# A filter network's third weight stacked on 128 partitions, x loaded in pieces, and a chunk evicted earlier, in a two-block transformer kernel

## The reference

```
h = x * (1 + sc1) + sh1;   z = h @ w_in + b_in
u, v = gelu(z[:, 0:1024]), gelu(z[:, 1024:2048]);   v = layer_norm(v)
f = sin(freq * (feats @ w1 + b1))          # 256 x 33 @ 33 x 64
f = sin(freq * (f @ w2 + b2))              # 64 x 64
f = f @ w3                                 # 64 x 4096: direction, order, 1024 channels
filt = f.reshape(256, 2, 2, 1024) * window[:, None, None, :]
spectrum(order n) = rfft of filt[:, 0, n] forwards and filt[:, 1, n] backwards
```

## Time and profile before

| | |
|---|---|
| median of 3 runs | 2676.2 us (2675.57 to 2677.15) |
| the profiled execution | 2677.23 us |
| its span in the trace | 2675.9 us |
| PE busy | 2630.5 us (98%) |
| DVE busy | 1840.9 us (69%) |
| ACT busy | 1291.8 us (48%) |
| moved by DMA | 598.48 MB, mean 224 GB/s |

### The profile page before, as it was taken

How to read it: one execution, slowest core, us unless ns; L and a number is a source line. 1 busy time by engine, 2 the same in 40 slices (tenths; PEclk the granted TensorE clock), 3 DMA queues, 4 the chain that set the end, 5 groups by cost and what they waited for, 6 DMA issues and landing times.

```text
span 2675.9 us, 32016 instructions
## 1 busy us (share of the span) xinstructions
PE 2630.5 (98%) x12713; PEld 2194.3 (82%) x12713; DVE 1840.9 (69%) x1919; ACT 1291.8 (48%) x1566; POOL 37.5 (1%) x62
## 2 busy tenths in 40 slices
PE   6999999999999999999999999999999999999999
PEld 2679988888888888888888888888888888988887
DVE  6878879887886654577776867765554665566565
ACT  2345544444444444555555544444444565545463
POOL 0000000000000000000000000000000000000000
PEclk9999999999999999999999999999999999999999
DMA  9999778888878865565556555555565556634554
GB/s 296 343 327 336 266 253 305 287 302 314 313 248 276 278 204 188 182 215 191 199 188 195 192 184 192 185 189 189 190 212 189 189 187 164 187 115 153 199 183 142
DMA packets 295800, 598.48 MB, mean 224 GB/s; under 512 B 21716, under 2 KB 46943, under 8 KB 285551
## 3 DMA queue, kind: packets, MB, share of 16 engines
q1 hardware_dynamic: 285952, 561.56, 62.6%
q0 software_dynamic: 5552, 25.23, 2.8%
q10 hardware_dynamic: 4158, 9.79, 1.0%
HBM read 586.05 MB, written 10.49 MB: 223 GB/s over the span
## 4 chain that ended last, share of the span: by engine, by line
PE 95%; DVE 3%; ACT 1%; DMA 1%; issue 1%; SPq 0%; ACTq 0%; DVEq 0%
PE ps L893 27%; PE ps L895 26%; PE ps L894 26%; PE ps L1016 2%; PE ps L1000 2%; PE ps L1002 2%; PE ps L1003 2%; PE ps L1092 1%; DVE w_lo L2261 1%; DMA raw<-in_w_ada 1%; PE ps L1435 1%; PE ps L1437 1%; PE ps L1436 1%; DVE ada_acc L2289 1%; PE ps L1085 0%
## 5 line engine op out<-in xcount | busy, mean ns | idle before, releaser
L2261 DVE TENSOR_TENSOR w_lo<-raw,w_hi 128x1024 fp32r<-128x1024 f32 x870 | 1051.3, 1222 | 698.4 <-ACT w_hi L1581 696.4
L1581 ACT CAST w_hi<-raw 128x1024 fp32r<-128x1024 f32 x870 | 909.0, 1051 | 1070.0 <-PE ps L895 964.9
L893 PE MATMUL ps<-w_lo,x_hi 128*128 128x512 f32 x2592 | 1020.8, 394 | 7.1 <-DVE x_lo L2416 3.4
L895 PE MATMUL ps<-w_hi,x_lo 128*128 128x512 f32 x2592 | 1011.9, 390 | 0.0
L894 PE MATMUL ps<-w_hi,x_hi 128*128 128x512 f32 x2592 | 1011.4, 390 | 0.0
L893 PEld LDWEIGHTS ps<-w_lo,x_hi 128*128 128x128 f32 x2592 | 488.5, 188 | 112.5 <-DVE x_lo L2416 5.0
L895 PEld LDWEIGHTS ps<-w_hi,x_lo 128*128 128x128 f32 x2592 | 488.2, 188 | 102.6
L894 PEld LDWEIGHTS ps<-w_hi,x_hi 128*128 128x128 f32 x2592 | 488.5, 188 | 100.7 <-issue 1.4
L2289 DVE SCALAR_TENSOR_TENSOR ada_acc<-raw,cond,ada_acc 128x2048 f32<-128x2048 f32 x64 | 150.1, 2346 | 1.0 <-DVE ada_acc L2289 0.5
L893 PE MATMUL ps<-w_lo,pooled_hi 128*128 128x512 f32 x384 | 150.2, 391 | 0.0
L895 PE MATMUL ps<-w_hi,pooled_lo 128*128 128x512 f32 x384 | 149.5, 389 | 0.0
(11 more groups left out here) (408 smaller groups left out, 2223.7 us busy)
## 6 DMA issues: line engine op xcount, KB each, us to landing
raw<-in_w_m SPq DMA_DIRECT2D x128, 1024.0 KB, 5.1
raw<-in_w_in SPq DMA_DIRECT2D x72, 1024.0 KB, 6.4
raw<-in_w_ada SPq DMA_DIRECT2D x64, 1024.0 KB, 5.5
raw<-in_pool_w_in SPq DMA_DIRECT2D x64, 1024.0 KB, 5.2
raw<-in_w_ada SPq DMA_DIRECT2D x64, 512.0 KB, 5.7
raw<-in_pool_w_out SPq DMA_DIRECT2D x32, 1024.0 KB, 5.0
raw<-in_ple_w_gate SPq DMA_DIRECT2D x32, 1024.0 KB, 5.1
raw<-in_mla_w_in SPq DMA_DIRECT2D x24, 1024.0 KB, 5.1
```

The lines of the kernel that those rows point to most:

```text
L893: mm(bank, xh, wl, start=start, stop=False)
L895: ins = mm(bank, xl, wh, start=False, stop=stop)
L1581: nc.scalar.copy(by_ktile(st, w_hi[st.half_slot(j, half)][:, 0:n]), raw_half(st, j, half)).then_inc(hi_split, 1)
L2261: tt(by_ktile(st, w_lo[slot][:, 0:n]), raw_half(st, j, half), by_ktile(st, w_hi[slot][:, 0:n].bitcast(F32)), ALU.subtract).then_inc(lo_spl ...
```

## The change

- The third weight `w3` now has 128 partitions of 2048 columns: the forward half on partitions 0 to 63, the backward half on 64 to 127. The second weight `w2`, its bias and the frequencies are loaded twice side by side, so that the second layer comes out on 128 partitions, its lower and upper halves equal. ACT takes three sines: `hid_dif` (upper half negated, in two operations) and `hid_sum`. Each filter product is then one matmul per 128 tokens with 128 rows, for all four chunks. `filter_weights` and `w3_sum` go.
- ACT issues ten small loads and one of `w3`; POOL waits for the ten, then issues the other half of `w3`, `window` and `dft`. Each of the four loads of x waits for one more of DVE's adds (`ada_added` 2 to 5) in place of `w3`.
- DVE's order up to the end of group 0 changes.
- In `in_vu` DVE evicts chunk 2 ahead of the last three pieces of w_ada, `gelu(2)` and the rounding of the table go behind the fourth half piece of `in_h` on ACT, and the table's split goes into `in_h` on DVE. The order of the loads is as before.

```diff
-    ("in_vu", 1, [("w", "awaaa")]), ("in_h", 2, A2), ...
+    ("in_vu", 1, [("wa", "waaa")]), ("in_h", 2, A2), ...
...
-    w3 = at("w3", 148, [4 * W1])
-    w3_sum = at("w3_sum", 120, [2 * W1])
+    w3 = at("w3", 156, [2 * W1])
...
+        pool.wait_ge(hidden_in, 160)
+        pool.dma_start(w3[HID:P, :], a["hy_w3"][0][:, 2 * W1:4 * W1]).then_inc(w3_back_in, 16)
         for dst, src in matrices:
             pool.dma_start(dst, src).then_inc(matrices_in, 16)
-        pool.wait_ge(w3_in, 64)
...
         for c in range(4):
+            pool.wait_ge(ada_added, 2 + c)
             pool.dma_start(res[:, :, cols(c)], x_rows[:, :, cols(c)]).then_inc(x_loaded, 16)
...
-        pe.wait_ge(hidden_in, 96)
+        pe.wait_ge(hidden_in, 160)
...
-        mm(ps[0:HID, 0, 0:S], w2[0:HID, :], hid_arg[0:HID, :], start=True, stop=True).then_inc(hid_mm, 1)
+        mm(ps[:, 0, 0:S], w2[0:HID, :], hid_arg[0:HID, :], start=True, stop=True).then_inc(hid_mm, 1)
...
-                bwd = w3[0:HID, 2 * W1 + col:2 * W1 + col + CH]
-                if it == 0:
-                    mm(bank, hid_arg[0:HID, tokens], w3[0:HID, 0:CH], start=True, stop=False)
-                    ins = mm(bank, (hid_neg if d else hid_arg)[0:HID, tokens], bwd, start=False, stop=True)
-                else:
-                    part = bwd if d else w3_sum[0:HID, col:col + CH]
-                    ins = mm(bank, hid_arg[0:HID, tokens], part, start=True, stop=True)
+                ins = mm(bank, (hid_dif if d else hid_sum)[:, tokens], w3[:, col:col + CH], start=True, stop=True)
...
-        pe.wait_ge(w3_in, 64)
+        pe.wait_ge(w3_in, 16)
+        pe.wait_ge(w3_back_in, 16)
...
-        pe.wait_ge(w3_ready, 2)
...
-            (w2[0:HID, :], a["hy_w2"][0], hidden_in), (hid_rows[0:1, :], a["hy_b1"], hidden_in),
-            (hid_rows[1:2, :], a["hy_b2"], hidden_in), (hid_rows[2:3, :], a["hy_freq"], hidden_in),
-        ]
+        ] + [(dst[:, HID * n:HID * (n + 1)], src, hidden_in) for n in range(2) for dst, src in (
+            (w2[0:HID, :], a["hy_w2"][0]), (hid_rows[0:1, :], a["hy_b1"]), (hid_rows[1:2, :], a["hy_b2"]), (hid_rows[2:3, :], a["hy_freq"]))]
...
-        for part in range(4):
-            columns = slice(part * W1, (part + 1) * W1)
-            act.dma_start(w3[0:HID, columns], a["hy_w3"][0][:, columns]).then_inc(w3_in, 16)
+        act.dma_start(w3[0:HID, :], a["hy_w3"][0][:, 0:2 * W1]).then_inc(w3_in, 16)
...
-                nc.scalar.activation(hid_neg[0:HID, :], hid_arg[0:HID, :], ACT.Sin, scale=-1.0)
-            nc.scalar.activation(hid_arg[0:HID, :], hid_arg[0:HID, :], ACT.Sin).then_inc(hid_sin, 1)
+                nc.scalar.activation(hid_dif[0:HID, :], hid_arg[0:HID, :], ACT.Sin)
+                nc.scalar.activation(hid_dif[HID:P, :], hid_arg[HID:P, :], ACT.Sin, scale=-1.0)
+                nc.scalar.activation(hid_sum[:], hid_arg[:], ACT.Sin).then_inc(hid_sin, 1)
+            else:
+                nc.scalar.activation(hid_arg[0:HID, :], hid_arg[0:HID, :], ACT.Sin).then_inc(hid_sin, 1)
...
-        run_at(ST["in_vu"], 0, {2: lambda: gelu(0), 4: lambda: (gelu(1), round_dft(0), gelu(2))})
+        run_at(ST["in_vu"], 0, {2: lambda: gelu(0), 4: lambda: gelu(1)})
...
             if n == 0:
+                gelu(2)
                 gelu(3)
                 spectrum_store(2)
                 spectrum_store(3)
+                round_dft(0)
...
         add_first(0, 2)
+        filter_part(0, 0)
         add_first(0, 3)
-        filter_part(0, 0)
-        filter_weights()
+        filter_part(0, 1)
+        add_first(0, 4)
         positions()
-        add_first(0, 4)
-        filter_part(0, 1)
         add_first(0, 5)
         group_rest(0, 0)
         vectors_turned()
+        filter_part(1, 0)
         add_first(0, 6)
-        filter_part(1, 0)
+        filter_part(1, 1)
         add_first(0, 7)
-        filter_part(1, 1)
...
-        run_at(ST["in_vu"], 0, {0: lambda: vu_out(0), 2: lambda: vu_out(1), 4: lambda: (split_dft(0), vu_out(2))},
-               lambda i, n: (2, n))
+        st = ST["in_vu"]
+        vu_out(0)
+        rest_unit(st, 0, 0)
+        add_ada(st, 0, 1, 2, 0)
+        vu_out(1)
+        rest_unit(st, 0, 2)
+        vu_out(2)
+        for n in range(1, 4):
+            add_ada(st, 0, 2 + n, 2, n)
...
-        run_at(ST["in_h"], 0, {4: lambda: vu_out(3), 8: sgu_norm, 12: lambda: conv_sides(0)}, lambda i, n: (2, 4 + n))
+        run_at(ST["in_h"], 0, {4: lambda: vu_out(3), 6: lambda: split_dft(0), 8: sgu_norm, 12: lambda: conv_sides(0)}, lambda i, n: (2, 4 + n))
```

More of the change, by code:

```diff
@@ L82 @@
     ("first", 1, [("aaaaaawaa", "")] + [("aawaawaawaa", "")] * 2 + [("aawaawawaaaw", "www")]),
-    ("in_vu", 1, [("w", "awaaa")]), ("in_h", 2, A2), ("in_h2", 1, A2), ("in_g", 4, [("wwa", "wwaa"), ("ww", "wwa")]),
+    ("in_vu", 1, [("wa", "waaa")]), ("in_h", 2, A2), ("in_h2", 1, A2), ("in_g", 4, [("wwa", "wwaa"), ("ww", "wwa")]),
     ("mix", 1, [("ww", "a")] * 8), ("w_o", 1, [("ww", "wawa")] * 4),
@@ L210, in block_kernel @@
     window = at("window", 140, [2, W1])
-    w3 = at("w3", 148, [4 * W1])
-    w3_sum = at("w3_sum", 120, [2 * W1])
+    w3 = at("w3", 156, [2 * W1])
     feats = at("feats", 164, [S])
     w1 = at("w1", 165, [HID])
-    w2 = at("w2", 165.25, [HID])
+    w2 = at("w2", 165.25, [2 * HID])
     hid_arg = at("hid_arg", 166, [S])
@@ L339, in block_kernel @@
     hid_cols = at("hid_cols", 206.9375, [3])
-    hid_rows = at("hid_rows", 168, [HID])
-    hid_neg = at("hid_neg", 169, [S])
+    hid_rows = at("hid_rows", 168, [2 * HID])
+    hid_dif = at("hid_dif", 169, [S])
+    hid_sum = at("hid_sum", 170, [S])
     COL = dict(pool_scale=0, q_norm=32, kv_norm=36, sgu_b=40, c=48, ln1_g=64, ln1_b=80, skip=100)
@@ L389, in block_kernel @@
     filt_win = sem("filt_win")
-    w3_ready = sem("w3_ready")
+    w3_back_in = sem("w3_back_in")
     c_in = sem("c_in")
@@ L1040, in _ @@
         nc.tensor.transpose(ps[:, 4, 0:KT], c_rows[0:KT, :], ident[0:KT, 0:KT]).then_inc(c_turned, 1)
-        pe.wait_ge(hidden_in, 96)
-        nc.tensor.transpose(ps[0:HID, 1, 0:3], hid_rows[0:3, :], ident[0:3, 0:3])
+        pe.wait_ge(hidden_in, 160)
+        nc.tensor.transpose(ps[:, 1, 0:3], hid_rows[0:3, :], ident[0:3, 0:3])
         mm(ps[0:HID, 0, 0:S], w1[0:EMB, :], feats[0:EMB, :], start=True, stop=True).then_inc(hid_mm, 1)
         pe.wait_ge(hid_sin, 1)
-        mm(ps[0:HID, 0, 0:S], w2[0:HID, :], hid_arg[0:HID, :], start=True, stop=True).then_inc(hid_mm, 1)
+        mm(ps[:, 0, 0:S], w2[0:HID, :], hid_arg[0:HID, :], start=True, stop=True).then_inc(hid_mm, 1)
         def turn_vectors():
@@ L2353, in hidden @@
             if layer == 0:
-                then(nc.vector.tensor_copy(hid_cols[0:HID, :], ps[0:HID, 1, 0:3]))
-            bias = hid_cols[0:HID, layer:layer + 1]
-            freq = hid_cols[0:HID, 2:3]
-            then(tsc(hid_arg[0:HID, :], ps[0:HID, 0, 0:S], bias, freq, ALU.add, ALU.mult))
-            sine_arg(hid_arg[0:HID, :], hid_n[0:HID, :], layer).then_inc(hid_red, 1)
+                then(nc.vector.tensor_copy(hid_cols[:], ps[:, 1, 0:3]))
+            part = slice(0, P if layer else HID)
+            bias, freq = hid_cols[part, layer:layer + 1], hid_cols[part, 2:3]
+            then(tsc(hid_arg[part, :], ps[part, 0, 0:S], bias, freq, ALU.add, ALU.mult))
+            sine_arg(hid_arg[part, :], hid_n[part, :], layer).then_inc(hid_red, 1)
         def filter_part(it, d):
@@ L2368, in filter_part @@
             tt((h_sum, h_dif)[d][:], ps[:, bank:bank + 2, :], window[:, :, c * CH:(c + 1) * CH], ALU.mult).then_inc(filt_win, 1)
-        def filter_weights():
-            dve.wait_ge(w3_in, 64)
-            fwd, bwd = w3[0:HID, CH:2 * W1], w3[0:HID, 2 * W1 + CH:4 * W1]
-            tt(w3_sum[0:HID, CH:], fwd, bwd, ALU.add).then_inc(w3_ready, 1)
-            dve.wait_ge(w3_ready, 1)
-            tt(bwd, fwd, bwd, ALU.subtract).then_inc(w3_ready, 1)
         def rope_angles():
```

## The result

The changed kernel takes 2663.4 us (median of 5 runs, 2662.4 to 2667.1), the kernel before 2676.4 (5 runs, 2675.6 to 2677.7): a ratio of 0.9950, interval 0.9939 to 0.9961, a gain of 13.0 us. The prediction said 2663. The end came out right, but partly by two errors that cancel: 1.5 us less was won at the front than the sum has, and 2.4 more behind it. To that extent the number is luck.

A forecast was written before the change was run, and what follows sets the result against it. PE, busy for 98% of 2675.9 us, was taken to bound the kernel, with gains only in the front before 211 us. 14.4 - 1.5 + 1.0 - 0.2 = 13.7 us off 2676.2 gave 2662.5, stated as 2663; range 2656 to 2671.

The forecast's parts named there:

- (a): Front, small loads: four more on ACT's queue, landing at 8.5 us (bounds 7.5 to 11.5), no loss.
- (b): Front, w_ada piece: in by 10 us, DVE's add no longer waits, filter starts at 20.0 instead of 27.2, 7.2 us.
- (c): Front, POOL's held loads: dft lands near 22 us, wanted at 23.5, no cost, cover 1.5 us.
- (d): Filter products: eight passes for sixteen, clock rising within them, ending at 26 instead of 41.2, another 8 us.
- (e): Rest up to group_sum(0): start 48.1 instead of 62.5, 14.4 us for (a) to (e), less 1.5 for missing covers.
- (f): Later products: 128 rows end the lower-clock spell from 102 us sooner, 1 us (0 to 3).
- (g): Third chunk evicted first: DVE stands some 3 us for bias 2; cost 0.2 us, gain none.
- Loads bind: Rival, chance 0.2: loads at 122 us and on come only 10 us earlier; gain 10, time 2666.
- The eviction pays: Rival, chance 0.1: bias 2 lands in time for the third eviction, 3 to 5.5 us more, time 2658.
- Matrices late: Rival, chance 0.1: POOL at 112 GB/s, dft lands at 31, gain 6 to 9 us, time 2668.
- Slower: Rival, chance 0.04: dft so late that DVE frees no slots and SP loads nothing; 2681 at 70 GB/s.
- no effect: Rival, chance 0.06: two or three of the other rivals together leave under 5.4 us of gain.

The follow-up runs named there:

- before_held: Kernel before the change with one edit: POOL waits for the six small loads ahead of window and dft; 2671.8 us, ratio 0.9978.
- pool_at_once: Changed kernel with POOL's loads not held: window and dft at once, then the back half of w3; 2667.8 us.
- half_height: Changed kernel with the filter's products over the lower 64 rows only, the backward half of the filter left out; 2666.8 us.
- first_twice: Changed kernel with the first chunk's filter products each issued twice, sixteen passes of 128 rows; 2663.5 us.
- window_pos: Changed kernel with a separate semaphore for window and the positions step ahead of DVE's add 4; 2664.7 us.
- combined_order: Changed kernel with the edits of window_pos and bias_early, plus ACT's copy of spectrum(0,1) ahead of the first rounding; 2658.4 us.
- bias_early_again: The same program as bias_early, measured once more; 2659.3 us.
- bias_early: Changed kernel with the third chunk's bias issued on SP's queue ahead of the last two pieces of in_vu; 2658.6 us.
- evict_old: Changed kernel with only the third-chunk part undone (in_vu pattern, ACT's and DVE's order as before); 2661.9 us.

## Why the prediction was right, point by point

**(a) Early loads: no loss was wrong, by its own bound.** The small loads landed at 10.1, not 8.5, ten of them as late as six with POOL's matrices beside them. With six and POOL held (before_held) they were in at 8.96, so what the hold gives, the four more loads took. PE's layer then ends at 11.4, DVE's first argument starts at 11.63 instead of 10.4: 1.2 us of loss, as the text had set it (each us beyond about 9 costs one). The view of the queues between 5 and 10 us says who took the place: SP's queue moved 1.80 MB there, 0.59 before.

**(b) The piece of w_ada: right, 6.0 us instead of 7.2**, the difference being (a)'s. No wait ahead of the add, and the filter starts at 21.27. before_held confirms the cause: that one wait takes DVE's stand for w_ada from 6.71 to 1.01. pool_at_once loses the gain in another way, 5.4 us by the small loads and only 1.7 by w_ada, so with ten small loads the hold is worth more for them than for the piece.

**(c) POOL's queue: its cover was gone.** The queue started 1.6 us later than the text had it, with (a), and dft landed at 25.4 instead of 22, 13.6 us after its issue: DVE, which wanted it at about 25.0, stood 2.99 us in all, of which only the last 0.4 is the DMA's alone. `filter_part(0, 0)` was released by a DMA and not by PE, as the text named for wrong. The price was small because PE was late too.

**(d) Half the passes: right in kind, 7.5 us instead of 8.** The level rose within the 128-row products, and not within as many 64-row ones (half_height: 7.1 us for eight passes at the lower level, then 6.5 for the spectrum). The Trainium skill (TensorE: Matmul & The Clock Gate, What's actually happening) has the clock follow how busy PE is; PE is busy for all of 24 to 28 us in both kernels, the changed one and half_height, and only one of them is at the upper level when the next spectrum begins. Here the measurement decides against the rule read alone. But "of which the following steps keep what they can" was little: with the level up the number of passes is worth nothing at `group_sum(0)` (first_twice: sixteen end in time for the positions), and with half the passes the level is worth 0.7 us at most (half_height).

**(e) Up to `group_sum(0)`: the margin of 1.5 was too small.** Predicted 14.4 less 1.5, measured 11.4. The positions were ready at 34.0, not 31.4: their small vectors were in at 31.9 (0.5 missing of the bound of 1.5), but add 4, which stands ahead of them on DVE, ended 2.6 late, by (a), (c) and 0.98 us of waiting for w_ada. The level fell in that pause (1.7 us, nowhere in the sum). From there to the ACT copies ahead of the sum PE does not stand, so this is the path of the changed kernel itself. Yet window_pos takes it away and wins 0.5. The step that failed is the landing of the first weight piece, "at about 35", for which no working is given. It was issued at 22.5, when add 2 had freed its slot, 1.0 us later than the text has it, and landed 15.4 us later, at 37.9, where the text allows 13.5. In that stretch the DMA engines ran at a share of 1.05 and 376 GB/s: 5.8 MB came in, pieces of w_ada ahead of it and POOL's matrices beside it. The text had named this piece and priced its wait at 0.7; it came 2.9 later than that, and the sum stands 13 us behind its landing in the forecast (35 and 48.1) as in the profiles of the changed kernel, window_pos and combined_order (37.9 and 51.1, 37.6 and 50.6, 37.9 and 50.7). In the sum it is the term "14.4 less 1.5" that was 1.5 too large.

**(f) Later products: the size was off, 3.2 us instead of 1, and the reason was wrong.** Between `group_sum(0)` and `group_sum(1)` 3.3 us were won, by two spectra at the upper level. In the chain of the kernel before they stand as:

```profile
64.47 5.24 PE ps L1092 x8
78.42 5.30 PE ps L1092 x8
```

After the change both take 3.7 (at 52.90 and 65.66). I had put the gain into the later spell, from 102 on, which did not shorten (now 88 to 96, at 0.56 to 0.59). And the height did not do it: half_height has the same 3.7 with 64 rows. Nor did shorter pauses of PE: those ahead of `group_sum(0)` and of the second of the two spectra are 1.2 and 1.3 us in both kernels. What did is not settled. After 60 us the kernel before was at the lower level at 64, 78 and 102 us, the changed one only at 88 to 96; but the place moves between executions of one program (bias_early_again), and first_twice has its spectrum at 52.65 at the lower level (5.24) and still the changed kernel's end. The 3.3 us are therefore shown as a matter of the level, in these two profiles, and not as an effect of any one edit. They are not all chance either. From `group_sum(0)` to `group_sum(2)` the two kernels with the old products and order take 70.2 us (before) and 72.0 (before_held); the eleven profiles of the changed kernel and its variants take 65.3 to 68.5. Which part of the change does it stays open; DVE's two operations of `filter_weights`, x in pieces and the closed hole in the loads were not tried apart.

**(g) The third eviction: right.** DVE stands 3.01 us for bias 2 (3.3 forecast), PE's pause is 4.75 us instead of 4.41, and undone the part gives back 0.4 (0.2 forecast; 0.2 to 0.9 over all profiles). bias_early confirms the bound "no wait at all, 3 better" with 3.0, and PE does keep its level over the shorter pause, as the "up to 2.4 more" had it; at the end of the span that was worth between nothing and 3.3 us.

**The rivals.** *Loads bind* came nearest: not as the end's limit, but at `group_sum(0)`, which no reordering tried here brought below 50.6. *The eviction pays* is what bias_early makes of it, 2658.6 for 2658 named. *Matrices late* was true by 0.4 us of wait, not by its price. *Slower* and *no effect* are ruled out by the 13.0 us, more than twice the 5.4 that were to be told from nothing.

**The sum** again, by what the profiles show: 11.4 to `group_sum(0)` (forecast 12.9), 3.3 to the next and 0.1 to the third (1.0), less 0.4 to chunk 4 (0.2) and 0.5 behind it (nothing): 13.9 for 13.7, the difference of the two profiled executions (2677.23 and 2663.37).

## What to carry to other kernels

When several things come free at the front of a kernel, look for the load that was issued last of those that many steps need: removing waits ahead of it gains next to nothing (window_pos and combined_order took away PE's waits of 1.4 us for the positions and 2.1 for ACT's copy and brought the sum forward by 0.5, where two profiles of one program, bias_early, differ by 1.0). Covers of one or two us should not be counted on together: here those of the matrices, the positions and the first weight piece were all gone, and only that of x held. Give each load's landing a working of its own, from the volume in flight with it (5.8 MB at 376 GB/s for the weight piece). And where a change adds a wait for a small load, ask what stands before it on its queue: moving one 256 KB bias ahead of two 1 MB pieces was worth 3.0 us more, beside a change of 13.0.

## What the runs showed of the hardware that was not expected

- The height of a product changed how soon the clock rose: 7.1 us of 64-row passes (and 14 in before_held, 20.5 to 34.5) were at 0.9 us a pass from first to last, while 128-row passes in their place were at the upper level when they ended. What of a product counts, its rows or what they switch, no run here tells.
- The place of the later spells at 1.2 GHz differs between executions of one program (52 to 60 or 88 to 96 us), and each is worth 1.6 to 2.8 us (by the distances between the sums in evict_old, bias_early and bias_early_again). The runs of one variant spread by 2 to 8 us (bias_early 2654.5 to 2662.6), those of the kernel before by 3; differences of 2 us between two variants' medians are therefore not read here, and the trace decides.
- Taking POOL's matrices away from six small loads made these land only 1.0 us earlier (10.0 and 9.0, before_held): most of the freed place went to SP's queue, 677 packets in 5 to 10 us where there were 303, against 202 and 169 of ACT's. Ten small loads without the matrices landed at 10.1 (931 packets of SP's, 220 of ACT's), ten with them (pool_at_once) at 15.5: beside the matrices the four more (and the other loads of `w3`) cost 5.5 us, without them 1.1.
